# Two shift chunks of the conditioning: cast in the queue of GpSimd, or loaded uncast by SyncE in eight pieces and cast by VectorE and ScalarE

## The reference, cut to what matters

```python
mod = silu(c) @ w_ada + b_ada                       # (B, 6 * 1024), float32
sh1, sc1, g1, sh2, sc2, g2 = split(mod, 6)
u = rmsnorm(h, norm1_w) * (1 + sc1) + sh1
proj = u @ w_in                                     # (B, S, 8192): q, k, v, gates, conv
# retention (k and v of earlier chunks reach a chunk through a state), short convolution,
# gated merge, residual; then u2 = rmsnorm(h) * (1 + sc2) + sh2 and a squared-ReLU MLP
```

## Time and profile before

| | |
|---|---|
| median of 3 runs | 1303.54 us (1303.44 to 1304.1) |
| the profiled execution's own time | 1304.79 us |
| its span, slowest core (core 0) | 1303.2 us |
| spans of all cores | 1295.8 to 1303.2 us |
| TensorE matmul busy | 1217.7 us, 93% of the span |
| VectorE, ScalarE, GpSimd busy | 516.2, 432.3, 485.4 us |
| HBM read | 175.54 MB |

### The profile page before, as it was taken

The page is one execution under the profiler, slowest core; times in us unless marked ns, Lnnn a source line. Parts: engine busy times, 40 slices in busy tenths (PEclk is TensorE's granted clock), DMA queues, the critical chain, the costliest instruction groups (busy, mean ns, idle before and its releaser), DMA issues.

```text
span 1303.2 us, 18942 instructions; the slowest of 8 cores (1295.8 to 1303.2 us)
## 1 busy us (share of the span) xinstructions
PE 1217.7 (93%) x6198; PEld 582.1 (45%) x6320; DVE 516.2 (40%) x957; ACT 432.3 (33%) x732; POOL 485.4 (37%) x501
## 2 busy tenths in 40 slices
PE   2577999999999999999899999999999999999997
PEld 0243444444444455555444444454444444444443
DVE  5465466776422267776217333420000450000145
ACT  2363454222212147777532223343320113331011
POOL 1268000100100068887654222256640136663012
PEclk9888999999999999999999999999999999999999
DMA  9949810576744220000682222994645549845223
GB/s 170 207 124 192 147 48 1 80 114 93 101 67 65 32 51 1 2 2 1 100 144 81 97 99 81 177 211 66 94 69 79 118 136 184 131 65 92 46 90 129
DMA packets 86016, 123.30 MB, mean 95 GB/s; under 512 B 4640, under 2 KB 69152, under 8 KB 85920
## 3 DMA queue, kind: packets, MB, share of 16 engines
q0 software_dynamic: 67632, 70.26, 37.6%
q1 hardware_dynamic: 15984, 43.43, 10.2%
q10 hardware_dynamic: 2304, 8.39, 1.7%
HBM read 175.54 MB, written 16.78 MB: 148 GB/s over the span
## 4 chain that ended last, share of the span: by engine, by line
PE 86%; DMA 5%; DVE 3%; issue 2%; ACT 2%; POOL 1%; DVEq 0%; POOLq 0%; ACTq 0%; SPq 0%
PE PS L306 83%; DMA ring<-w_in 3%; PE PS L481 1%; DMA scr<-x_main 1%; DVE AR L985 1%; PE PS L1023 1%; DMA scr<-x_pre 1%; ACT Z L489 1%; DVE Y L468 0%; ACT X L489 0%; DVE scr L441 0%; POOL Z L1123 0%; PE PS L950 0%; PE PS L947 0%; ACT Y L457 0%
## 5 line engine op out<-in xcount | busy, mean ns | idle before, releaser
L306 PE MATMUL PS<-X,ring 128*128 128x512 bf16 x2506 | 566.7, 380 | 12.7 <-ACT scr L1047 5.9
L306 PEld LDWEIGHTS PS<-X,ring 128*128 128x128 bf16 x2560 | 249.9, 98 | 309.4 <-issue 16.1
L306 PE MATMUL PS<-ring,Z 128*128 128x512 bf16 x869 | 207.2, 389 | 15.9 <-DVE scr L564 6.0
L306 PEld LDWEIGHTS PS<-ring,Z 128*128 128x128 bf16 x896 | 88.8, 100 | 124.0 <-issue 27.6
L1286 DVE TENSOR_TENSOR AR<-PS,G_t 128x512 f32<-128x512 f32 x16 | 11.1, 692 | 294.9 <-PE PS L306 294.9
L1267 ACT ACTIVATE scr<-PS 128x512 f32<-128x512 f32 x128 | 76.3, 597 | 140.8 <-PE PS L306 89.5
L306 PE MATMUL PS<-Y,ring 128*128 128x512 bf16 x506 | 119.5, 379 | 0.3
L306 PE MATMUL PS<-ring,X 128*128 128x512 bf16 x493 | 115.3, 379 | 3.4 <-DVE AR L985 2.6
L306 PE MATMUL PS<-ring,Y 128*128 128x512 bf16 x501 | 112.7, 379 | 0.6
L1270 POOL TENSOR_TENSOR Z<-scr 128x512 bf16<-128x512 f32 x64 | 67.0, 1050 | 37.9 <-ACT scr L1267 32.0
L1270 POOL TENSOR_TENSOR Y<-scr 128x512 bf16<-128x512 f32 x64 | 66.6, 1041 | 36.9 <-ACT scr L1267 31.4
(11 more groups left out here) (167 smaller groups left out, 1342.9 us busy)
## 6 DMA issues: line engine op xcount, KB each, us to landing
ring<-w_ff POOLq DMA_DIRECT2D x32, 1024.0 KB, 9.1
ring<-w_in POOLq DMA_DIRECT2D x17, 1024.0 KB, 21.8
ring<-w_ada POOLq DMA_DIRECT2D x12, 1024.0 KB, 11.9
scr<-x_main SPq DMA_DIRECT2D x23, 512.0 KB, 7.2
scr<-h1s SPq DMA_DIRECT2D x32, 256.0 KB, 4.9
y<-scr ACTq DMA_DIRECT2D x16, 512.0 KB, 4.6
h1s<-scr SPq DMA_DIRECT2D x12, 512.0 KB, 5.5
scr<-x_pre SPq DMA_DIRECT2D x8, 512.0 KB, 13.7
```

The costliest lines, as they stand in the source:

```text
L306: S.op("pe", lambda e: e.matmul(out, lhsT, rhs, start=start, stop=stop), reads=list(lkeys) + list(rkeys), writes=[okey])
```

## The change

The list `chunks` loses the two shift chunks, and the ring is held at three. In their place SyncE's queue loads the 1024 x 1024 block as it is, in float32, in eight pieces of 128 rows (512 KB each), into the eight rows of Z, right behind the first four tiles of `x_pre`. VectorE casts the even pieces and ScalarE the odd ones into X rows 4 to 7. `mod_Tk` then takes two matmuls from each piece, one for each bank, in the order of the pieces, and evicts as before.

```diff
-        chunks = [adak(1, 0), adak(1, 1), adak(0, 0), adak(0, 1), wchunk(w_in, 0, 512)]
+        chunks = [adak(1, 0), adak(1, 1), wchunk(w_in, 0, 512)]
...
-        rstate = {"load": 0, "use": 0, "limit": 5}
+        rstate = {"load": 0, "use": 0, "limit": 3}
...
-                if i < 4:
+                if i < 2:
...
-        def mod_Tk(v, col, bks, tmp, tmpk):
-            for kh in range(2):
+        def mod_Tk(v, col, bks, tmp, tmpk, pieces=None):
+            if pieces:
+                for i, (ap, keys) in enumerate(pieces):
+                    for n in range(2):
+                        mm(pa[bks[n]], ("pa", bks[n]), crep[:, i, :], [("crep", i)], ap[:, n * 512:(n + 1) * 512], keys, i == 0, i == 7)
+            for kh in range(2 if not pieces else 0):
...
         pair_load()
         pair_load()
+        a_raw = [Z[:, i, :].bitcast(F32) for i in R8]
+        a_pcs = [(X[:, 4 + i // 2, (i % 2) * 1024:(i % 2 + 1) * 1024], [("X", 4 + i // 2, 2 * (i % 2)), ("X", 4 + i // 2, 2 * (i % 2) + 1)]) for i in R8]
+        for i in R8:
+            dma("sp", a_raw[i], w_ada[i * 128:(i + 1) * 128, 0:1024], [], XK("Z", [i], range(4)), ("adr", i))
+
+        def a_cast(i):
+            ap, keys = a_pcs[i]
+            if i % 2:
+                S.op("act", lambda e: e.copy(out=ap, in_=a_raw[i]), reads=XK("Z", [i], range(4)), writes=keys)
+            else:
+                S.op("dve", lambda e: e.tensor_copy(out=ap, in_=a_raw[i]), reads=XK("Z", [i], range(4)), writes=keys)
+
...
-        mod_Tk(0, 8, [2, 3], tmp_m, tmp_mk)
+        for i in R8:
+            a_cast(i)
+        mod_Tk(0, 8, [2, 3], tmp_m, tmp_mk, a_pcs)
```

## The result

Over 17 runs each the changed kernel takes 1306.49 us (median) and the kernel before 1303.85: a ratio of 1.002, 95% interval 1.0012 to 1.0027. It is slower by 2.6 us, just at the bound of what I called no change, and just above my range (1306.4). In some executions of either kernel the cores of one die show a lower granted clock and take far longer (1510 us once for the kernel before); ratios, and all means, medians and counts further down, leave these out. T is the time at which the eighth piece has landed, read from the start of its cast, and R the start of the first rotation.

A forecast was written before the change was run, and what follows sets the result against it. Bound: the chain through `w_in` and tiles 4 and 5 to the first rotation R, 55.6 us on core 0. T 45.5 plus 10.2 gave R 55.7, +0.1 us, so 1303.6 us; range 1301.2 to 1306.4.

The forecast's parts named there:

- no change: For the whole kernel's time: a measurement within about 0.2%, 2.6 us, counts as this; chance 0.58.
- R is the time that counts: At the first rotation, 55.6 us on core 0: its shift reaches the end of the span, nothing absorbs it.
- (1), the price of the pieces: Shift load: 1024 packets go from 0.19 to 0.202 us each, 0.8 us more of the 16 engines.
- (2), the mixing: Both queues full from 24 us: gain 1.10 (ends 1.05, 1.26), so T = 45.5 and `w_in` about 2 us before the last packet.
- My first rival: Mixed load up to T: no gain by mixing, T 47.6, R 57.8, +2.2 to +3.2 us, 1305.7 to 1306.7; chance 0.27.
- The rule of the Trainium skill: On DMA queues: different engines' transfers run on the same 16 DMA engines; issuing from several saves only issue time.
- (3), from T to R: Last cast, matmul, VectorE's diagonal and bias, evictions, squares of tiles 4 and 5, rotation: R = T + 10.2.
- (4) to (7), the covers: Around the first rotations: seven casts, issues, first `p_k` matmuls (by half a us) and later loads add nothing to the chain.
- The cores: Across cores: 0 and 7 set the time; fast ones lose more (core 1: R 52.7 to about 55) but have room.

The follow-up runs named there:

- e2: The changed kernel with the `w_in` chunk issued only when the eighth piece has landed: ratio 1.0051, median 1310.7 us.
- e6: The changed kernel with the squares of tiles 4 and 5 on ScalarE ahead of the four evictions of p_tpart(0): ratio 1.0005.
- e8: The changed kernel measured again, unaltered, on one chip with the kernel before, for the spans of all cores: median 1305.96 us, ratio 1.001.
- e7: The changed kernel with a `w_ada` chunk (512 packets of 2 KB) in place of the `w_in` chunk (1024 of 1 KB): ratio 1.0013.
- e3: The changed kernel with tiles 4 and 5 of `x_pre` loaded ahead of the pieces and their squares ahead of ScalarE's casts: ratio 1.0031.
- e5: Half of the change: first shift chunk by the ring as in the kernel before, the second as four uncast pieces by SyncE: ratio 0.9989.
- e1: The changed kernel's eight pieces, but loaded and cast by GpSimd's queue straight into the X rows, ahead of the `w_in` chunk: ratio 0.9999.
- e4r: Repeat of e4, the kernel before with tiles 4 and 5 loaded early: ratio 1.0023.
- e10: Against e5 (four pieces by SyncE): tiles 4 and 5 right behind the pieces, squares ahead of the evictions; ratio 1.004, median 1311.2 us.
- e4: The kernel before with tiles 4 and 5 of `x_pre` loaded right behind tiles 0 to 3, squares ahead of the shift's matmuls: ratio 1.0009.

## Why the prediction was wrong, step by step

*R is the time that counts.* Right for the mean over the cores: where R moves by 3 us and more, the mean span follows by 0.5 to 0.9 of it. But not one for one, as I had put it ("nothing absorbs it"), and not to be read from a pair of cores, as I did: on core 0 of the profiled pair R moved by 2.8 us (55.6 to 58.4) and the span fell by 5.3. In the profiled pair R moved by 5.0 us, the first ring load behind it by 5.0 too (89.9 to 94.9), the last square that waits for an `x_main` tile only by 3.1 (119.8 to 122.9, means over cores): the wait that ended at 120.9 us on core 0 got shorter. In it the engines carried about as many bytes in each 4 us as before (188 to 261 GB/s on core 0 before from 100 to 124 us, 178 to 252 on core 5 after from 104 to 128); why the tile that is waited for came earlier among them is open.

*(1), the price of the pieces.* Right: e2 has them alone at 316 to 346 GB/s, for the 325 that the price came from, and T at 39.9 where the same sum gives 24 + 14.5 + 1.0 = 39.5.

*(2), the mixing.* This is the step that failed: the factor 1.10 in T = 24 + 22.6/1.10 + 1.0. I read a gain of 1.05 to 1.26 out of three windows. In two of them the packets were not one for one (878 against 249, 704 against 261), so one queue had run short at times; the third (375 against 372, 1.08) had both at work, but no `w_in` packets. The mixed queues of the changed kernel show 1.04 while both are full, and nothing of it is left at the end of the load: T is 47.6 by the sum without a gain, and 49.1 (48.2 to 48.3 in e6 and e8) was measured. So 2.1 us of the 3.6 by which T was late are the gain that I assumed, and the rest, 0.6 to 1.5, is not in the sum at all. My first rival had the mechanism (chance 0.27), with T = 47.6 and 1305.7 to 1306.7 us. That the result lies in its range is in part luck: T was later than it had, and less of R's shift arrived. The rule of the Trainium skill beside it ("DMA: Bandwidth & Descriptors", "Issuing engines are not separate DMA queues") is borne out but for these 4%: the second queue brought the load to no earlier end.

What the rest is stays open. The sum takes from core 0 of the kernel before what is loaded by 24 us (1.69 MB on q1), and the cores differ in that: in the changed kernel core 0 had 1.80 MB and T = 48.1, core 5 had 1.60 and T = 50.2. With each core's own megabytes put into the sum (an estimate), T is late by 1.2 us on the mean of the changed kernel, 0.9 in e8, 1.1 in e6, 2.2 in e7 and 2.7 in e3. It is late by 1.2 in e2 too, where the pieces have the engines to themselves: the mean of its cores had 1.97 MB by 24 us, which hides it in the 39.9 for 39.5. Where GpSimd's queue ends last, the landing of `w_in` is over the same sum by 0.4 us in the kernel before, 0.1 in e5 and 0.9 in e1. So the rest is largest where SyncE's queue is the last, but e1 comes near it, and e2 has it without any mixing. That single engines get behind and are then waited for is what the windows at 61% and 28% suggest; the views do not tell the engines apart, and no run tests it.

*(3), from T to R.* Right to 0.1 us: 10.3 for 10.2 on core 5, with each step, and 10.3 on the mean of the cores. e3 and core 1 of e6 show its next limit, TensorE's first eight matmuls at T + 9.

*(4) to (7), the covers.* They held: no cast but the last is on the chain, the second rotation is 3.0 us behind the first, tiles 4 and 5 are not waited for. This last cover is thinner than I had it, since `w_in`, for which they wait, landed at 46.8 and not at 43.5; where their squares are put earlier (e6) it is gone on half of the cores.

*The cores.* I had the slowest, 0 and 7, in view and gave the cores with room no weight. Before, four cores had tile 5 at 51 us and four at 54 to 56; now all wait for the eighth piece, so the four early ones lost 6 to 8 us of R and the others 2.3 to 3.4. The time suffers less than the mean of the cores from that: the median time lies 5.6 to 6.1 us above the mean span in the kernel before (three jobs), and 4.4 to 5.2 in the kernels in which T sets R (the changed one, e2, e3, e6, e7, e8).

## What to carry to other kernels

Moving a load to a second queue did not make it earlier: count the packets that both queues hold, pair them one for one, price each as if alone, and expect a us or more on top (0.9 to 2.7 here where SyncE's queue was the last). In these runs the queue with the most packets left ended last, so the transfer that the chain needs first must not be on it. And a load that is behind in one queue may be ahead of what waits for it in another engine's list: the order of landings, and not the sum of the bytes, was what the change gave up (the shift at 49 in the place of 39 us).

## What the runs showed of the hardware that I had not expected

The granted clock of TensorE can stay at 0.81 for some 140 us. On core 4 of e4r it is 0.81 from 76 us on, 0.50 from 81 to 84, and 0.81 again until 234 us; on core 0 of e10 it falls from 1.00 to 0.81 within 58 to 60 us and is back at 1.00 by 219. In windows of the trace as short as 1 us it is 0.81 too, so it is not a mixture of the two levels, 1.2 and 2.4 GHz, between which it lies. TensorE was at 1.00 and busy throughout 71 to 75 us before it fell on core 4, and busy for 59.2 of the 60 us in which it came back. In e4r cores 4 and 5 have it and 6 and 7, on the same die, do not.

Putting tiles 4 and 5 early (e4, e4r, e10) left 66 of 224 cores at a mean clock below 0.972 over the span, most at 0.96, against 9 of 584 for the kernel before in the same jobs, and those cores end 10 to 12 us later than the others. The cause is not shown. An earlier R is not it: e10 has the most such cores, 44 of 80, at an R of 54.2, which is that of the kernel before. Nor is a small spread of R over the cores enough: it is 1.2 us in e10, but 2.3 in the changed kernel, which has none, against 2.6 in e4. A reordering of work can so lose more by the clock than it wins, and one profiled execution may show either.
